# Layer b's probabilities times values as three products of rounded and rest parts

## What is computed

```
p = jax.nn.softmax(logits, axis=-1)        # [128 queries, 12 heads, keys], keys up to the block's end
return jnp.einsum('bqhk,bqkd->bqhd', p, vg)
```

## Time and profile before

| | |
|---|---|
| median of 3 runs | 1694.58 us (1693.11 to 1694.98) |
| profiled execution | 1694.56 us, span 1692.8 us |
| TensorE busy | 1663.4 us, 98% |
| VectorE busy | 916.9 us, 54% |
| ScalarE busy | 572.4 us, 34% |
| GpSimd busy | 1053.0 us, 62% |
| thirteen slots of layer b | from about 1360 to 1584 us of the span |

### The profile page before, as it was taken

How to read it: one execution, slowest core, us unless ns; L and a number is a source line. 1 busy time by engine, 2 the same in 40 slices (tenths; PEclk the granted TensorE clock), 3 DMA queues, 4 the chain that set the end, 5 groups by cost and what they waited for, 6 DMA issues and landing times.

```text
span 1692.8 us, 22289 instructions
## 1 busy us (share of the span) xinstructions
PE 1663.4 (98%) x8073; PEld 1364.6 (81%) x8073; DVE 916.9 (54%) x1411; ACT 572.4 (34%) x990; POOL 1053.0 (62%) x779
## 2 busy tenths in 40 slices
PE   7999999999999999999999999999999999999997
PEld 5897997888878888888888888887878777777785
DVE  5323948782445222221247997998475784443416
ACT  5331248330422100100144445756131345553203
POOL 7676754476647766766774889782577544333563
PEclk9999999999999999999999999999999999999999
DMA  6333333223343323333233332221423321121221
GB/s 207 125 102 121 104 100 125 96 79 100 100 149 94 92 93 95 99 100 100 81 117 101 99 100 90 77 83 54 162 72 106 95 75 51 51 74 51 75 87 50
DMA packets 191274, 162.10 MB, mean 96 GB/s; under 512 B 9684, under 2 KB 187472, under 8 KB 190672
## 3 DMA queue, kind: packets, MB, share of 16 engines
q1 hardware_dynamic: 190984, 160.84, 30.5%
q10 hardware_dynamic: 200, 0.06, 0.0%
HBM read 155.60 MB, written 4.23 MB: 94 GB/s over the span
## 4 chain that ended last, share of the span: by engine, by line
PE 92%; DVE 4%; ACT 2%; POOL 1%; issue 1%; DMA 0%; DVEq 0%; SPq 0%; ACTq 0%
PE g_bank L888 65%; PE g_bank L905 7%; PE g_bank L915 6%; PE t_bank L1465 2%; PE t_bank L1475 2%; PE g_bank L1369 1%; PE t_bank L1205 1%; PE t_bank L1237 1%; PE t_bank L1287 1%; PE t_bank L1308 1%; PE g_bank L1351 1%; PE t_bank L1454 1%; PE t_bank L949 1%; PE t_bank L1445 1%; DVE t_bank L2647 0%
## 5 line engine op out<-in xcount | busy, mean ns | idle before, releaser
L751 POOL TENSOR_TENSOR w_lo<-w_raw,w_hi 128x512 fp32r<-128x512 f32 x392 | 541.1, 1411 | 8.2
L738 POOL TENSOR_SCALAR w_hi<-w_raw 128x2048 fp32r<-128x2048 f32 x98 | 192.6, 1965 | 497.4 <-issue 214.0
L888 PE MATMUL g_bank<-x_hi,w_hi 128*128 128x512 f32 x1248 | 494.8, 396 | 0.2 <-DVEq L2222 0.2
L888 PE MATMUL g_bank<-x_hi,w_lo 128*128 128x512 f32 x1248 | 486.0, 389 | 0.0
L888 PE MATMUL g_bank<-x_lo,w_hi 128*128 128x512 f32 x1248 | 486.0, 389 | 0.0
L888 PEld LDWEIGHTS g_bank<-x_hi,w_hi 128*128 128x128 f32 x1248 | 234.4, 188 | 52.1 <-issue 4.4
L888 PEld LDWEIGHTS g_bank<-x_hi,w_lo 128*128 128x128 f32 x1248 | 234.3, 188 | 49.2
L888 PEld LDWEIGHTS g_bank<-x_lo,w_hi 128*128 128x128 f32 x1248 | 234.5, 188 | 48.5 <-issue 1.7
L2647 DVE SCALAR_TENSOR_TENSOR t_bank<-hc,cols,t_bank 128x512 f32<-128x512 f32 x280 | 187.0, 749 | 4.7 <-DVE hc L2631 2.8
L799 POOL TENSOR_TENSOR w_lo<-w_raw,w_hi 128x512 fp32r<-128x512 f32 x104 | 134.3, 1324 | 68.1 <-ACT w_hi L1868 68.1
L888 PE MATMUL g_bank<-y_hi,w_hi 128*128 128x512 f32 x332 | 130.9, 394 | 0.0
(11 more groups left out here) (458 smaller groups left out, 2907.3 us busy)
## 6 DMA issues: line engine op xcount, KB each, us to landing
w_raw<-w_gate_up SPq DMA_DIRECT2D x44, 512.0 KB, 5.0
w_raw<-a_w_in SPq DMA_DIRECT2D x44, 512.0 KB, 4.5
w_raw<-b_w_in SPq DMA_DIRECT2D x38, 512.0 KB, 4.3
w_raw<-w_in SPq DMA_DIRECT2D x28, 512.0 KB, 4.8
w_raw<-w_kv SPq DMA_DIRECT2D x16, 512.0 KB, 4.4
w_raw<-w_out_mix SPq DMA_DIRECT2D x16, 512.0 KB, 6.3
w_raw<-w_down SPq DMA_DIRECT2D x16, 512.0 KB, 3.9
w_raw<-a_w_out SPq DMA_DIRECT2D x16, 512.0 KB, 4.0
```

What stands on the lines that cost most here:

```text
L738: nc.gpsimd.tensor_scalar(w_hi[:, par], w_raw[:, par], 1.0, 0.0, ALU.mult, ALU.add).then_inc(pool_chain, 1)
L751: last = nc.gpsimd.tensor_tensor(w_lo[:, par, s], w_raw[:, par, s], w_hi[:, par, s].bitcast(F32), ALU.subtract)
L888: last = nc.tensor.matmul(g_bank[:, 2 * pair + f, 0:n], ww[:, k0 + k, ws], xk, start=(k == 0 and q == 0), stop=(k == kt - 1 and q == 2))
```

## The change

The values product becomes three rounded products in the place of a plain one. For that `vB` is split once: ScalarE writes `vB_hi`, VectorE the difference `vB_rest` (while the projection's bank is still held, so VectorE frees that bank now), and in slot 0 `vB_lo`, the rounded rest. Of each turned tile ScalarE writes `pTB_hi` (a rounded copy, announced by `uT_hi`, with no wait for its own end), and VectorE then writes `pTB_lo` as the bank's content less `pTB_hi`; VectorE's signal frees the bank and tells TensorE that the tile is there. In VectorE's program these subtractions (`rest_of_turned`) stand at the head of slot n, before the new unit's logits are read. `y0_lo` moves to another place in memory, and the two semaphores for stores become one.

```diff
--- before.py
+++ after.py
@@ -372,7 +372,9 @@
         qiT = at("qiT", [P, IH // 2, T], rY + 24 * KB)
         kB = at("kB", [P, T], rY + 32 * KB)
         kiT = at("kiT", [P, T], rY + 34 * KB)
-        vB = at("vB", [P, TT, P], rY + 36 * KB)
+        vB_hi = at("vB_hi", [P, TT, P], rY + 36 * KB, F32R)
+        vB_lo = at("vB_lo", [P, TT, P], rY + 30 * KB, F32R)
+        vB_rest = at("vB_rest", [P, TT, P], rK + 4 * KB)
         W_OF = [(qb + 1) * P for qb in range(TT)]
         M_AT = [0, P, 3 * P, 6 * P]
         mask = at("mask", [P, 10 * P], rY + 38 * KB)
@@ -384,9 +386,10 @@
         rring = at("rring", [P, 2, T], rN + 2 * KB)
         pB2 = [at(f"pB2_{i}", [P, T], o) for i, o in enumerate((rN + 2 * KB, rN + 4 * KB, rN + 6 * KB, rY + 34 * KB))]
         pB = at("pB", [P, 4, T], rK)
-        pTB = at("pTB", [P, TT, 4 * P], rY + 24 * KB)
+        pTB_hi = [at(f"pTB_hi{i}", [P, 4 * P], o, F32R) for i, o in enumerate((rY + 24 * KB, rY + 26 * KB, rY + 28 * KB, rN))]
+        pTB_lo = [at(f"pTB_lo{i}", [P, TT, 4 * P], o, F32R) for i, o in enumerate((rS + 16 * KB, rM))]
         y0_hi = at("y0_hi", [P, 4, T], rY, F32R)
-        y0_lo = at("y0_lo", [P, 4, T], rM, F32R)
+        y0_lo = at("y0_lo", [P, 4, T], rY + 38 * KB, F32R)
         ym_hi = at("ym_hi", [P, MH_, T], rM + 8 * KB, F32R)
         ym_lo = at("ym_lo", [P, MH_, T], rK + 8 * KB, F32R)
         onat = at("onat", [P, 8, T], rS + 8 * KB)
@@ -411,6 +414,10 @@
         def pT_at(u):
 
             return 0 if u == units_of(SLOT_OF[u])[0] else UNITS[u - 1][0] + 1
+
+        def pT_parts(u, kt):
+
+            return pTB_hi[pT_at(u) + kt][:], pTB_lo[SLOT_OF[u] >= 8][:, pT_at(u) + kt, :]
 
         def a_parts(k):
 
@@ -475,7 +482,7 @@
         mem2_n, m2_hi, m2_lo, mvar = sem("mem2_n"), sem("m2_hi"), sem("m2_lo"), sem("mvar")
         sg_ready, ga_ready, ff_hi, ff_lo = sem("sg_ready"), sem("ga_ready"), sem("ff_hi"), sem("ff_lo")
         kv_ready, kv_moved, gs_ready = sem("kv_ready"), sem("kv_moved"), sem("gs_ready")
-        out_done = [sem("out_done0"), sem("out_done1")]
+        out_done = sem("out_done")
 
         glu_s, conv_done = sem("glu_s"), sem("conv_done")
         glu_done, a_hi, tap_chain, pconv_done, taps_begun = sem("glu_done"), sem("a_hi"), sem("tap_chain"), sem("pconv_done"), sem("taps_begun")
@@ -490,6 +497,7 @@
         b_in, dist_ready, qi_ready = sem("b_in"), sem("dist_ready"), sem("qi_ready")
         relu_ready, acc_done = sem("relu_ready"), sem("acc_done")
         um_ready, ue_ready, up_ready, uT_ready, uo_ready = sem("um_ready"), sem("ue_ready"), sem("up_ready"), sem("uT_ready"), sem("uo_ready")
+        uT_hi = sem("uT_hi")
         on_act, on_pool, on_dve, in_brow = sem("on_act"), sem("on_pool"), sem("on_dve"), sem("in_brow")
         fin_dve, fin_act, hg_ready = sem("fin_dve"), sem("fin_act"), sem("hg_ready")
         ln_cent, ln_sq, ln_sq_used, ln_sums = sem("ln_cent"), sem("ln_sq"), sem("ln_sq_used"), sem("ln_sums")
@@ -704,9 +712,8 @@
                     sp.wait_ge(on_pool, OUT_BY_ACT.index(i) + 1)
                 else:
                     sp.wait_ge(on_dve, sum(q not in OUT_BY_ACT for q in range(i + 1)))
-                sp.dma_start(out[0, m * P:(m + 1) * P, h * T:(h + 1) * T], onat[:, i, :]).then_inc(out_done[i % 2], 16)
-            for done_sem in out_done:
-                sp.wait_ge(done_sem, 16 * 4)
+                sp.dma_start(out[0, m * P:(m + 1) * P, h * T:(h + 1) * T], onat[:, i, :]).then_inc(out_done, 16)
+            sp.wait_ge(out_done, 16 * 8)
 
 
         @block.gpsimd
@@ -1472,7 +1479,9 @@
                 b = bank(TASKS[f"bV{u}"])
                 pe.wait_ge(uT_ready, sum(UNITS[x][0] + 1 for x in range(u + 1)))
                 for kt in range(qb + 1):
-                    last = nc.tensor.matmul(b, vB[:, kt, :], pTB[:, pT_at(u) + kt, :], start=(kt == 0), stop=(kt == qb))
+                    hi, lo = pT_parts(u, kt)
+                    for q, (vv, pp) in enumerate(((vB_hi, hi), (vB_hi, lo), (vB_lo, hi))):
+                        last = nc.tensor.matmul(b, vv[:, kt, :], pp, start=(kt == 0 and q == 0), stop=(kt == qb and q == 2))
                 last.then_inc(t_ready, 1)
 
             pe.wait_ge(b_in, 1)
@@ -2099,9 +2108,8 @@
             j = JOBS["b_v"]
             act.wait_ge(w_used, j + 1)
             g = g_bank[:, 2 * (j % 2):2 * (j % 2) + 2, :].rearrange("p b (m c) -> p (b m) c", c=WC)
-            copy(vB[:], g[:, :, 0:P])
+            copy(vB_hi[:], g[:, :, 0:P])
             link(copy(wi[:], g[:, :, P:P + IH]))
-            act.nop().then_inc(g_free[j % 2], 1)
             act.nop().then_inc(b_in, 2)
             def relus(g):
 
@@ -2129,9 +2137,7 @@
                 for kt in range(UNITS[u][0] + 1):
                     i = TASKS[f"bT{u}"] + kt
                     b = ready(i)
-                    link(copy(pTB[:, pT_at(u) + kt, :], b))
-                    act.nop().then_inc(t_free[BANK[i]], 1)
-                    act.nop().then_inc(uT_ready, 1)
+                    copy(pT_parts(u, kt)[0], b).then_inc(uT_hi, 1)
 
             def values(u):
                 qb, hg = UNITS[u]
@@ -2867,6 +2873,9 @@
             link(v.tensor_copy(mask[:, 0:P], dist[:, T - P:T]))
             link(v.memset(mask[0:64, 64:P], FAR))
             dve.wait_ge(b_in, 3)
+            j = JOBS["b_v"]
+            g = g_bank[:, 2 * (j % 2):2 * (j % 2) + 2, :].rearrange("p b (m c) -> p (b m) c", c=WC)
+            done(v.tensor_tensor(vB_rest[:], g[:, :, 0:P], vB_hi[:].bitcast(F32), ALU.subtract), g_free[j % 2])
 
             def accumulate(g):
 
@@ -2916,6 +2925,14 @@
                     p = p_unit(u, i)
                     ins = v.tensor_scalar(p, p, ast[:, u, 2, i:i + 1], None, ALU.mult)
                 ins.then_inc(up_ready, 1)
+
+            def rest_of_turned(u):
+
+                for kt in range(UNITS[u][0] + 1):
+                    r = TASKS[f"bT{u}"] + kt
+                    dve.wait_ge(uT_hi, sum(UNITS[x][0] + 1 for x in range(u)) + kt + 1)
+                    hi, lo = pT_parts(u, kt)
+                    done(v.tensor_tensor(lo, ready(r), hi.bitcast(F32), ALU.subtract), uT_ready, t_free[BANK[r]])
 
             def y_product(k):
                 a = qB[:, k, :] if k < AH else qmT[:, k - AH, :]
@@ -2942,6 +2959,9 @@
             for n in range(N_SLOTS):
                 if n == 0:
                     accumulate(5)
+                    link(v.tensor_scalar(vB_lo[:], vB_rest[:], 1.0, None, ALU.mult))
+                for u in units_of(n - 2):
+                    rest_of_turned(u)
                 for u in units_of(n):
                     unit(u)
                 if n in (1, 3, 5):
```

## The result

The changed kernel takes 1699.52 us (median of 8 runs, 1698.15 to 1702.26) beside 1694.81 (1693.11 to 1695.0): ratio 1.0031, 95% interval [1.0022, 1.004]. It is slower by 4.7; the forecast was 4.5 slower, 1699.0. The execution profiled took 1698.88, with a span of 1697.0.

What follows compares the result with a forecast made beforehand. TensorE, busy 1663.4 of 1692.8 us, was taken to bound the kernel. New waits of 9.8 for VectorE-freed banks, less 5.3 from shorter products, gave +4.5: 1694.6 to 1699.0 us, range 1695.3 to 1701.0.

Steps and rivals of the forecast that it cites:

- 0.176 each, 5.3 over 30: Values products on TensorE: three rounded ones at 0.227 a step replace each plain 0.857, giving back 0.176, 5.3 over 30.
- 1.13 after the end of ScalarE's copy: Turned bank before the logits: hand-over 0.14, subtraction 0.69, back to TensorE 0.30; before, 0.19 at most.
- A step of 1.00: VectorE frees successive turned banks every 1.00 us: operation 0.69 plus 0.31 for completion wait and two signals.
- I take 0.09, once per block: A plain TensorE product after a wait runs 0.09 us longer, its weight load being uncovered; counted once per block.
- Slot 7, "+0.40": Slot 7's block, its logits waiting for turned banks, was to end at 1501.06 against 1500.66: +0.40 us.
- rival 3: VectorE reaches the turned banks late, top-k rounds still queued; one more microsecond in each of eight blocks: 1707; chance 0.10.
- Slot 6: Slot 6's block, its logits waiting for turned banks, was to end at 1481.57 against 1480.64: +0.93 us.
- The first: Rival: VectorE's completion waits cost nothing, so its step is 0.69; +1.0, 1695.6, no change; chance 0.14.
- The second: Rival: logits don't wait because banks have room, so the 5.3 stay whole; 1689.3, faster; chance 0.06.

Runs made afterwards that it cites:

- x10: Changed kernel, but ScalarE frees the turned banks, their rest part is left out, and two store semaphores stay: 1688.81 us beside 1694.53, ratio 0.9966.
- x3: Changed kernel, but each subtraction frees its bank itself and VectorE waits only for a unit's last one: 1695.44 us beside 1693.76, ratio 1.001.
- x6: Changed kernel with top-k rounds spread 3, 3, 3, 4, 3 over slots 2 to 6 instead of 2, 3, 2, 4, 5: 1698.35 us beside 1694.68.
- x1: Kernel before with its plain products, but VectorE subtracts from and frees each turned bank; vB not split: 1703.64 us beside 1693.76, ratio 1.0055.
- x5: Changed kernel, but ScalarE copies banks out raw and frees them; rounding and subtraction follow from memory: 1689.1 us beside 1693.76, ratio 0.9973.

## Why the prediction was right, step by step

**Products, "0.176 each, 5.3 over 30".** Right: 0.227 a step, -0.71 in each of slots 10 to 12, -5.3 over the blocks of x10. The rate was read from the same form in another place of the trace, which is why it needed no bound of any width.

**Bank free "1.13 after the end of ScalarE's copy".** In slot 9 it was 1.04: 0.03 to VectorE's start (1537.80 + 0.60 = 1538.40, then 1538.43) where I had 0.14, 0.69, and 0.32 back to TensorE where I had 0.30.

**"A step of 1.00".** Measured 1.02, and three of them stand in a full block: +0.06. That it is the wait for completion, with the signals sent behind it, is shown by x3, with 0.60.

**"I take 0.09, once per block" for the uncovered weight load.** Nearly nothing: in slot 9 the last bank was free at 1541.50 + 0.69 + 0.32 = 1542.51, and with 0.857 for the last logit the block would end at 1543.37, as it did. Together the small terms make -0.11 + 0.02 + 0.06 - 0.09, about -0.1 in slot 9; slots 2 to 5 and 8 were 0.1 to 0.2 under the forecast as well.

**Slot 7, "+0.40".** This step failed: +1.26. I had costed VectorE's part at nothing where it has idle time before the logits, from slots 2 and 5. I had not followed what the three subtractions in front do to VectorE's later work in slot 6: the four scalings started 4.8 later than before (1490.90, now 1495.71), GpSimd's batch only 3.4 (1491.93, now 1495.34), and so they fell into it. Being late by itself was not enough: four scalings of 1.41 from 1495.71 would have ended at 1497.1, well before 1500.4. x6 takes the overlap away and gets 1.0 back; its slot 7 is +0.25, again 0.15 under the forecast. This is the mechanism of rival 3 (VectorE late to the turned banks, one microsecond more in a block), in one block out of eight and for a reason the rival did not name. The Trainium skill states such a reason, in "SBUF — State Buffer", section "Who interferes with whom": VectorE's two-port modes, which `tensor_scalar` can enter, use a pair of ports shared with GpSimd, and one engine waits out the other; its operations with two inputs in memory contend with a GpSimd instruction that reads memory. The rows agree: four scalings 1.41 alone, 5.81 or 4.12 beside the batch; an operation with two inputs in memory 0.69 and 1.64; while the subtraction with one input in a bank kept its 0.68 beside GpSimd. That the ports are the reason no run here shows by itself.

**Slot 6** came 0.14 over the forecast: ScalarE's first turned copy ended 5.49 after the block's start instead of 5.20, after one of its memory copies had waited 0.47 for TensorE. The same copy waited 0.47 or 0.48 in x1, x3 and x6 and not in x10 (0.18), so it comes with VectorE freeing the banks; by what path was not tested.

So the sum was close (4.5 against 4.7) partly because six small overestimates, 0.8 together, stood against slots 6 and 7, 1.0 together. That they cancelled is luck; the mechanism, the step and the price of a hand-over are not.

**Rivals.** The first, a free completion wait, would have been +1.0; the step of 1.02 refutes it, and x3, which takes the waits out by an edit, lands at +1.7. The second, no waiting of the logits, is refuted by slot 9; x10 and x5 are what it would have looked like. The rule that the prediction set beside the first, from the Trainium skill's "VectorE: DVE Perf Modes", section "The DRAIN you can't avoid", says that a semaphore after each operation costs nothing. For a signal alone x3 agrees (0.60 with one behind each of the first three subtractions). For the engine's wait for its own completion, to which the prediction stretched it, it does not hold here: 1.02, for the same operation.

## What to carry to other kernels

When a second engine must read a buffer before it can be given back, count the hand-over once per chain and that engine's step with its completion wait once per buffer, and ask whether the product behind is shorter than that step. If the first engine can move the data out whole and free the buffer, the second can do its part from memory in its idle time: here that turned +4.7 into -6.1 with the same arithmetic (one top-k round was moved as well, worth 0.7 of it in the blocks). After any change that shifts one engine by microseconds, look at what its later work now runs beside.

## What was not expected of the hardware

- VectorE's scaling in memory ran 3 to 4 times longer beside GpSimd's batch (1.41 to 5.81 and 4.12 for four), in both kernels. The batch itself lost less, 5.30 and 5.69 for four of its operations against 4.96.
- Completion waits between VectorE's operations on a bank, with the signals behind them, cost 0.42 each (1.02 against 0.60); between ScalarE's raw copies 0.23 ((2.75 - 2.06) / 3).
- The changed kernel's runs spread over 4.1, those of x6 over 2.5. The scaling beside GpSimd does not explain it alone: x1 and x3 have it too and spread over 2.3 (5 runs) and 2.9 (11 runs).
